# Tile-by-tile tails over two weight units, a hold of GpSimd at three entries, and ScalarE's squares for two RMS norms

## The reference

```python
def rms_norm(x, g):
    y = x * lax.rsqrt(jnp.mean(x * x, axis=-1, keepdims=True) + RMS_EPS)
    return y * g

h = modulate(rms_norm(x, norm1_g), sh1, sc1)
x = x + g1 * token_mixer(h, ...)          # ends: att @ w_att_out, merged @ w_o
h = modulate(rms_norm(x, norm2_g), sh2, sc2)
x = x + g2 * (jnp.square(jax.nn.relu(h @ w1)) @ w2)
x = rms_norm(x, norm_f_g)                 # input of layer 0
# each layer: x = layernorm(ALPHA * x + mixer(x)); x = layernorm(ALPHA * x + experts(x))
```

## Time and profile before

| | |
|---|---|
| time, median of 3 runs | 1483.08 us (1480.79 to 1485.77) |
| profiled execution, its own time | 1474.82 us |
| its span | 1473.0 us |
| busy TensorE / VectorE / ScalarE / GpSimd | 91% / 59% / 50% / 44% of the span |
| mean granted TensorE clock | 0.952 of full |

### The profile page before, as it was taken

How to read it: one execution, slowest core, us unless ns; L and a number is a source line. 1 busy time by engine, 2 the same in 40 slices (tenths; PEclk the granted TensorE clock), 3 DMA queues, 4 the chain that set the end, 5 groups by cost and what they waited for, 6 DMA issues and landing times.

```text
span 1473.0 us, 17592 instructions
## 1 busy us (share of the span) xinstructions
PE 1336.8 (91%) x6128; PEld 1083.7 (74%) x6128; DVE 869.7 (59%) x1365; ACT 729.2 (50%) x1074; POOL 647.1 (44%) x528
## 2 busy tenths in 40 slices
PE   6899989999988799998987978999989888799996
PEld 3687767888866588886776767888767766778884
DVE  6564853544253552116755657877776746777777
ACT  4343444454643344444555515766645553366664
POOL 2799899977665699996200330000060023000000
PEclk9999999999999899999997979999999989699998
DMA  9956468654443455555421007778744300377782
GB/s 366 368 208 232 182 219 297 255 208 180 146 155 115 143 178 178 197 172 181 163 89 55 0 1 299 289 288 321 301 147 145 108 1 1 141 292 289 291 313 86
DMA packets 44478, 279.88 MB, mean 190 GB/s; under 512 B 5453, under 2 KB 8781, under 8 KB 12014
## 3 DMA queue, kind: packets, MB, share of 16 engines
q1 hardware_dynamic: 37426, 263.82, 48.9%
q10 hardware_dynamic: 6974, 15.05, 2.8%
HBM read 274.66 MB, written 4.19 MB: 189 GB/s over the span
## 4 chain that ended last, share of the span: by engine, by line
PE 58%; POOL 16%; DVE 11%; issue 6%; ACT 4%; DMA 3%; DVEq 2%; POOLq 0%; SPq 0%; ACTq 0%
POOL w_lo L603 16%; PE G L1105 9%; PE G L1107 9%; PE G L1106 9%; PE AC L1105 7%; PE AC L1107 7%; PE AC L1106 7%; DMA rel_scratch<-arena 1%; DVE mod L1924 1%; DMA w_raw<-w_stream 1%; PE AC L1524 1%; DVE sm L1871 1%; ACT w_hi L651 1%; PE AC L1544 1%; DVE x_sb L2233 1%
## 5 line engine op out<-in xcount | busy, mean ns | idle before, releaser
L603 POOL TENSOR_TENSOR w_lo<-w_raw,w_hi 128x512 fp32r<-128x512 f32 (+1 forms) x488 | 621.0, 1306 | 396.0 <-ACT w_hi L651 387.4
L651 ACT ACTIVATE w_hi<-w_raw 128x1024 fp32r<-128x1024 f32 x448 | 471.5, 1059 | 411.3 <-PE AC L1107 202.0
L1835 DVE TENSOR_TENSOR w_lo<-w_raw,w_hi 128x1024 fp32r<-128x1024 f32 x230 | 278.4, 1223 | 64.7 <-ACT w_hi L651 57.0
L1105 PE MATMUL AC<-w_hi,yT_hi 128*128 128x512 f32 x464 | 185.3, 399 | 18.1 <-POOL w_lo L603 16.2
L1107 PE MATMUL AC<-w_hi,yT_lo 128*128 128x512 f32 x464 | 181.9, 392 | 0.0
L1106 PE MATMUL AC<-w_lo,yT_hi 128*128 128x512 f32 x464 | 181.9, 392 | 0.0
L1105 PE MATMUL G<-w_hi,xT_hi 128*128 128x512 f32 x432 | 178.9, 414 | 2.7 <-DVE xT_lo L1841 2.6
L1107 PE MATMUL G<-w_hi,xT_lo 128*128 128x512 f32 x432 | 173.0, 401 | 0.0
L1106 PE MATMUL G<-w_lo,xT_hi 128*128 128x512 f32 x432 | 172.8, 400 | 0.0
L1105 PE MATMUL AC<-w_hi,xT_hi 128*128 128x512 f32 (+1 forms) x304 | 124.7, 410 | 13.7 <-POOL w_lo L603 7.1
L1105 PE MATMUL G<-w_hi,arena_r 128*128 128x512 f32 x320 | 128.0, 400 | 4.7 <-DVE arena L2672 3.4
(11 more groups left out here) (438 smaller groups left out, 1796.9 us busy)
## 6 DMA issues: line engine op xcount, KB each, us to landing
w_raw<-w_stream SPq DMA_DIRECT2D x152, 1024.0 KB, 4.8
w_raw<-w_expert SPq DMA_DIRECT2D x96, 1024.0 KB, 4.9
mod<-rows ACTq DMA_DIRECT2D x2, 2048.0 KB, 8.8
rel_scratch<-arena ACTq DMA_DIRECT2D x1, 3072.0 KB, 20.6
mod<-rows ACTq DMA_DIRECT2D x3, 476.0 KB, 5.5
x_sb<-x SPq DMA_DIRECT2D x1, 1024.0 KB, 9.4
arena<-const SPq DMA_DIRECT2D x1, 1024.0 KB, 8.4
mod<-gn_g ACTq DMA_DIRECT2D x1, 1024.0 KB, 15.0
```

The source lines that it names most:

```text
L603: i = pool.tensor_tensor(w_lo[:, k % SLOTS, cols], w_raw[:, raw, cols], w_hi[:, k % SLOTS, cols].bitcast(F32), ALU.subtract)
L651: act.activation(w_hi[:, k % SLOTS, :], w_raw[:, raw, :], ACT.Copy).then_inc(hi_ready, 1)
L1105: pe.matmul(out, xh, wh, start=start, stop=False)
L1835: dve.tensor_tensor(w_lo[:, k % SLOTS, :], w_raw[:, k % RAW, :], w_hi[:, k % SLOTS, :].bitcast(F32), ALU.subtract).then_inc(lo_ready, 1)
```

## The change

There are three edits.

1. **Tails over two units.** `down_tail` now covers the last two units instead of the last four. The two units before them go through `down`, which frees each after both tiles. In triples from the start of the last four units, the four sums (tile 0 first half, tile 0 second half, tile 1 first half, tile 1 second half) are complete after 6, 8, 14 and 16 before, and after 10, 12, 14 and 16 now. The four units are free after 10, 12, 15 and 16 before, and after 4, 8, 15 and 16 now.
2. **A hold of GpSimd.** At the entries of the MLP, layer 0 and layer 1, GpSimd makes unit 0's low part, and makes unit 1's only when tile 0 is normed (`h_ready` or `x_ready`).
3. **Squares on ScalarE.** At the norm before the MLP and at the final norm before layer 0, ScalarE squares each half of a residual row with an accumulated sum (`square`), released by the new count `res_ready`; VectorE adds the two sums and scales them. VectorE now also adds tile 1's first half to the residual before it norms tile 0. The flags are gone: layer 1's and the program's last norm use `ln_var`. At layer 0, ScalarE's high part of unit 3 comes after tile 1's square root.

```diff
+            for k in range(U_WO, U_MLP + RAW):
+                if k == U_MLP + 1:
+                    pool.wait_ge(h_ready, HALVES * (TOK + 1))
+                lo(0, k, UNIT // 2)
+            with pool.Fori(U_MLP // RAW + 1, U_LAYERS // RAW) as i:
                 lo_round(i * RAW, UNIT // 2)
...
+                for k in range(RAW):
+                    if k == 1:
+                        pool.wait_ge(x_ready, HALVES * (l * TOK + 1))
+                    lo(n, k, UNIT // 4)
...
+            def square(at, t, c):
+
+                act.wait_ge(res_ready, at + HALVES * t + c + 1)
+                act.activation(h_sb[:, t, c * NT:(c + 1) * NT], x_sb[:, t, c * NT:(c + 1) * NT], ACT.Square,
+                               accum_out=ssq[:, HALVES * t + c:HALVES * t + c + 1]).then_inc(sumsq_ready, 1)
...
             down_his(0, U_WO, T_MERGE, 4, mods_and_root)
+            square(0, 1, 0)
+            turn_hi_x(T_H2, 0)
+            square(0, 1, 1)
+            root(R_NORM2 + 1, var[1])
+            turn_hi_x(T_H2 + 2, 1)
...
                 r = l * LR + R_LAYERS
                 if l == 0:
                     his(2, SLOTS - 1, n)
+                    square(HALVES * TOK, 1, 0)
                 turn_hi_x(t + LT_X, 0)
-                his(SLOTS - 1, SLOTS, n)
+                if l == 0:
+                    square(HALVES * TOK, 1, 1)
+                else:
+                    his(SLOTS - 1, SLOTS, n)
                 root(r, var[1])
+                if l == 0:
+                    his(SLOTS - 1, SLOTS, n)
                 turn_hi_x(t + (LT_X + 2), 1)
                 act.wait_ge(x_ready, HALVES * (l * TOK + TOK))
...
-            def down_tail(n, k, first, amid=None, y_hi=yT_hi, y_lo=yT_lo):
+            def down_tail(n, k, first, y, y_hi=yT_hi, y_lo=yT_lo):
 
 
                 for t in range(TOK):
-                    for c in (0, 1):
-                        i = down_step(n, k, c, c, t, (0, 1), first and c == 0, False, y_hi, y_lo)
-                        if t == TOK - 1:
-                            i.then_inc(unit_used, 1)
-                    if t == 0 and amid:
-                        amid()
                     for j in (0, 1):
-                        for c in (2, 3):
-                            i = down_step(n, k, c, c, t, (j,), False, c == 3, y_hi, y_lo)
+                        for c in (0, 1):
+                            i = down_step(n, k, c, y + c, t, (j,), first and c == 0, c == 1, y_hi, y_lo)
                             if t == TOK - 1 and j == 1:
                                 i.then_inc(unit_used, 1)
...
-                    if 1 <= q <= pairs - (2 if tail else 0):
+                    if q >= 1:
                         pe.wait_ge(t_lo, t + 2 * q)
+                    if q == pairs and tail:
+                        down_tail(n, k + 2 * (q - 1), False, 2 * ((q - 1) % 2))
+                    elif q >= 1:
                         down(n, k + 2 * (q - 1), 2, q == 1, q == pairs, 2 * ((q - 1) % 2))
-                if tail:
-                    pe.wait_ge(t_lo, t + 2 * (pairs - 1))
-                    down_tail(n, k + 2 * (pairs - 2), pairs == 2, lambda: pe.wait_ge(t_lo, t + 2 * pairs))
...
             down(0, k + UP + 2, 2, False, False, 2)
             pe.wait_ge(t_lo, tn + 2 * TOK)
-            down_tail(0, k + 2 * UP, False, None, xT_hi, xT_lo)
+            down(0, k + 2 * UP, 2, False, False, 0, xT_hi, xT_lo)
+            down_tail(0, k + 2 * UP + 2, False, 2, xT_hi, xT_lo)
...
-            def rms_var(t):
-
-                aggregate(t)
-                dve.scalar_tensor_tensor(var[t], mv[:, t, 0:1], mv[:, t, 0:1], mv[:, t, 1:2], ALU.mult, ALU.add)
-                dep()
-                dve.tensor_scalar(var[t], var[t], 1.0, 1e-6, ALU.mult, ALU.add).then_inc(var_ready, 1)
-                dve.memset(mv[:, t, 0:1], 0.0)
-                dep()
+            def rms_var(at, t):
+
+                dve.wait_ge(sumsq_ready, at + HALVES * (t + 1))
+                dve.tensor_tensor(var[t], ssq[:, HALVES * t:HALVES * t + 1], ssq[:, HALVES * t + 1:HALVES * t + 2], ALU.add)
+                dep()
+                dve.tensor_scalar(var[t], var[t], 1.0 / D, 1e-6, ALU.mult, ALU.add).then_inc(var_ready, 1)
...
-            for t in range(TOK):
-                for c in range(HALVES):
-                    if t == 1:
-                        lo_x_half(T_H2, 0, c)
-                    acc_wait(ACC_WO, done(U_MLP), t, c)
-                    gated_residual(2, t, c)
-                    stats_half(t, c)
-                rms_var(t)
-                inverse_root(R_NORM2 + t, t)
+            def next_residual(g, n, n_done, t, c):
+
+                acc_wait(n, n_done, t, c)
+                gated_residual(g, t, c)
+
+            def scaled_and_shifted(t):
+
                 for c in range(HALVES):
                     scaled(t, c, norm2_row)
                     dep()
                     shifted(t, c, 3)
+
+            for t, c in ((0, 0), (0, 1), (1, 0)):
+                next_residual(2, ACC_WO, done(U_MLP), t, c)
+            rms_var(1, 0)
+            inverse_root(R_NORM2, 0)
+            scaled_and_shifted(0)
+            lo_x_half(T_H2, 0, 0)
+            next_residual(2, ACC_WO, done(U_MLP), 1, 1)
+            lo_x_half(T_H2, 0, 1)
+            rms_var(1, 1)
+            inverse_root(R_NORM2 + 1, 1)
+            scaled_and_shifted(1)
...
-            for t in range(TOK):
+
+            def final_scaled(t):
+
                 for c in range(HALVES):
-                    acc_wait(ACC_MLP, done(U_LAYERS), t, c)
-                    gated_residual(5, t, c)
-                    if t == 0:
-                        stats_half(0, c)
-                    else:
-                        lo_x_half(T_LAYERS + LT_X, 0, c)
-                if t == 0:
-                    rms_var(0)
-                    normed(R_FINAL, 0, "ln2_g", "ln2_b", x_ready)
-
+                    dve.scalar_tensor_tensor(x_sb[:, t, half(c)], x_sb[:, t, half(c)], var[t], row2["ln2_g"][:, half(c)], ALU.mult, ALU.mult).then_inc(x_ready, 1)
+
+            for t, c in ((0, 0), (0, 1), (1, 0)):
+                next_residual(5, ACC_MLP, done(U_LAYERS), t, c)
+            rms_var(1 + HALVES * TOK, 0)
+            inverse_root(R_FINAL, 0)
+            final_scaled(0)
+            lo_x_half(T_LAYERS + LT_X, 0, 0)
+            next_residual(5, ACC_MLP, done(U_LAYERS), 1, 1)
+            lo_x_half(T_LAYERS + LT_X, 0, 1)
+            rms_var(1 + HALVES * TOK, 1)
+            inverse_root(R_LAYERS, 1)
+            final_scaled(1)
...
-                last_stats()
-                normed(r, 1, "ln2_g", "ln2_b", x_ready)
+                if l:
+                    for c in range(HALVES):
+                        stats_half(1, c)
+                    ln_var(1)
+                    normed(r, 1, "ln2_g", "ln2_b", x_ready)
                 lo_x(tb + (LT_X + 2), 1)
-                for flag, value in ((about_zero, 0.0), (about_mean, 1.0), (norm_eps, 1e-5)):
-                    dve.memset(flag, value)
```

37 lines of the change are left out of this document (13 added, 24 removed).

## The result

The changed kernel has a median of 1470.28 us over ten runs (1461.34 to 1476.94). The kernel before, run beside it, brings its own median to 1479.62 us over ten runs. The ratio is 0.9917, 95% interval 0.9889 to 0.9944: some 12 us faster, between 8 and 16. The same kernel run again later gave 0.9939 (0.9910 to 0.9968), 9 us.

The account below looks back on a forecast made before the run. TensorE was taken to be busy nearly everywhere, losing time in short waits, 23.3 us of them for GpSimd's low parts. Terms of -0.9, -4.7, -1.1, -0.5 and -0.7 sum to -7.9: 1483.1 to 1475.2 us, range 1470.0 to 1480.5.

Parts of the forecast that it names:

- Attention output, -0.9: Attention output: both tiles of units 0 and 1 first shorten TensorE's 3.1 us wait; gain 0.9 us, bounds 0.3 to 2.7.
- w_o tail and MLP entry, -4.7: w_o tail to MLP entry: only unit 7 awaited, tile 0 normed sooner, unit 3 at 492.4; gain 4.7 us, bounds 3.8 to 6.2.
- I count nothing for it, since the norm sets the time there: w_o tail: one wait fewer may help TensorE's clock (matmul 0.79 us against 0.48), but it was put at zero.
- The hold removes GpSimd: MLP entry: with GpSimd held, VectorE's scale and shift of tile 0 take 3.1 us instead of 6.1.
- ScalarE's squares: MLP entry: squares of some 0.5 to 0.8 us each end within VectorE's next residual, except tile 1's first, costing 0.1.
- Layer 0's entry, -1.1: MLP tail and layer 0's entry: unit 3 starts at 693.7 instead of 694.80; gain 1.1 us, bounds 2.5 gained to 1.4 lost.
- Output projections, 0: Output projections: tile 0's sums wait for the last unit's low part in either order; no change, bounds 0.3 each way, twice.
- Layer 1's entry, -0.5: Layer 1's entry: two fewer instructions without flags and the hold; unit 3 at 1085.0 instead of 1085.46; bounds +0.5 and -1.5.
- The end, -0.7: Program's end: the last norm's chain is shorter without flags, with nothing running beside it; gain 0.7 us.
- full pieces: Rival, VectorE under GpSimd: each addition waits out a whole piece, 2.2 us; sum -1.6 us, 1481.5 us; chance 0.17.
- the hold did not starve TensorE: Rival, layers 0 and 1: twelve GpSimd pieces after release delay unit 3; +6.8 us at 1.47 a piece, 1490; chance 0.06.
- more than I count: Rival, several places: attention gains 2.7, entries 6.2 and 2.5, layer 1 1.5; sum -13.6 us, 1469.5 us; chance 0.11.

Follow-up runs that it names:

- the first profile: The unchanged kernel before, in the profile on which the forecast was made; its span is 1473.0 us.
- the other two: The unchanged kernel before, profiled a second and third time, one run each; measured 1477.65 and 1478.50 us.
- the filled tail: The kernel before with six and five unused identity products in the w_o tail's two waits; measured 1477.54 us, ratio 1.0000 (0.9966 to 1.0033).

## Why the prediction was wrong

The forecast of 1475.2 us is 4.9 above the median. Of this 3.5 us come from the base: it was made against a median of three runs, 1483.1, and ten have 1479.6. The other 1.4 are gain, 9.3 by these medians against 7.9; by the ratio the gain is 12 or 9 us.

- *Attention output, -0.9*: -1.0 and -1.7 against the first profile. The mechanism was right, and so was the dearer first addition. But the six profiles with the old tail stand at -0.1 to +1.6 there (mean 0.9) and the nine with the new one at -0.5 to -2.1 (mean -1.1), so it is worth about 2. Only the size was off; the first profile was 0.9 quicker here than the mean of its kind.
- *w_o tail and MLP entry, -4.7*: -5.6 against the first profile of before and about -8 against the other two. This is where the forecast failed. "I count nothing for it, since the norm sets the time there": the lower clock falls on the tail's last products, and the norm itself waits for these, for tile 0's sums and, through ScalarE's queue, for its root. The new tail has none of it (1.00 against 0.72 and 0.52). The term put at nothing measures 1.6 us against the first profile and 3.0 against the other two, by the filled tail. The sizes of the norm came out near: tile 0 was normed at 480.9, not 481.6, and unit 3 followed 0.8 us earlier than forecast.
- "The hold removes GpSimd": the 3.1 us for tile 0's scale and shift were right (2.9), but as a cause of the gain the step is wrong. Without the hold the place is 0.5 us slower and unit 3 0.4. What it gives tile 0 it takes from tile 1. That the sum came near is luck: the squares and the order of the residuals carried what the forecast gave to the hold.
- *ScalarE's squares* "end inside VectorE's next residual": right, and only because the tail frees slots early. I had given the parts no bond; alone the squares are worth nothing.
- *Layer 0's entry, -1.1*: -2.2 twice. The sizes: pieces of 0.81 us instead of 0.87 (12 of them, 0.7 us) and a release 0.4 us earlier. The squares carry this place (3.3 us), and pay there for the tail's +1.4.
- *Output projections, 0*: 0.0 at layer 0 between the first two profiles (the offset at 890 is that at 846). In the other profiles this stretch is 0.0 to 2.0 us slower, with the old tail and with the new, so one pair can't settle it.
- *Layer 1's entry, -0.5*: 0.1 by unit 3's start. 1.6 us come behind it, as a spell of the lower clock falls away, and go with a spell 50 us later; the forecast had no clock in this sum either.
- *The end, -0.7*: -0.7.
- The rivals: full pieces did not occur as a rule; the hold did not starve TensorE, though its waits of 1.64 and 0.62 us for low parts at layer 0 add up to more than the 2 us that I had named as a sign of being wrong; "more than I count" (-13.6) named the clock and is nearest to what the ratio gives.
- The sum: with the mean of before's three profiles at the w_o place (+1.6) and the two means at the attention output, the places without layer 0's mixer give -2.0 - 7.2 - 2.2 - 0.7 = -12.1 us; the ratios give 12 and 9. Against the first profile alone they give -9.5.

What stays open is what decides the clock in layer 0's mixer, whose fifteen profiles lie between -6.0 and +1.5 us. Values near both ends occur with the changed kernel itself. Whether the new tail moves the mean there is open too, and with it some 2 us of the gain. The effect of the lower clock in the w_o tail rests on one filled kernel, which agrees with the kernel with the tails alone.

## What to carry to other kernels

Test parts of a change together as well as apart: work moved to a second engine pays only if that engine's queue is free when the work arrives, and here another part of the change cleared it. A hold that keeps one engine off another moves a collision; it gains only what the later, displaced work does not lose. A gain can be a spell of the lower clock that moved, so follow it until the next spell is over. Profile the kernel before more than once before forecasting from one place: 2.5 us of this one's time at the decisive place, and its median by 3.5, were chance.
